# Where the sums of weights of the fifth and sixth slot are made, in a two-layer decoder trunk in fp32

## The chip, the cores and the metric

One core of one Trainium2 chip runs the kernel. The metric is the device time of one execution in microseconds (us). About 0.2% of it (1.8 us) is what a measurement of this kernel can tell from no change.

## What is computed

The reference is a decoder trunk with two layers on 256 tokens of width 1024, all in float32. Each layer is

```python
x = x + 0.5 * swiglu(rmsnorm(x, norm_ffn1[l]), ffn1_w_in[l], ffn1_w_out[l])
z = rmsnorm(x, norm_mix[l]) @ mix_w_in[l]
...
x = x + y @ mix_w_out[l]
x = x + 0.5 * swiglu(rmsnorm(x, norm_ffn2[l]), ffn2_w_in[l], ffn2_w_out[l])
```

where `swiglu(h, w_in, w_out)` is `(silu(g) * u) @ w_out` with a hidden width of 2816. The change lies in the last product of a layer, `(silu(g) * u) @ ffn2_w_out[l]`: 256 x 2816 by 2816 x 1024.

## The kernel before, in words

**Split products.** TensorE multiplies in a reduced format, so each fp32 operand is split into a rounded part and a remainder (`w_hi`, `w_lo`), and each product is three matmuls (`three`, lines 500 to 503). ScalarE makes the rounded parts (`w_hi` at L1016, or L1007 for a wide tile; `h_hi` at L1089; `s_hi` at L994), VectorE the remainders (`w_lo` at L1324 or L1319, `h_lo` at L1445, `s_lo` at L1348, `hs_lo` at L1452), each by a subtraction that needs the rounded part.

**Order of the work.** Each engine walks through the same half-steps h of a stage (4 to 4·UB+FT+1 with UB = 11 and FT = 22: the first 44 belong to the up product, the rest to the down product). At each h, VectorE does in this order: a `hidden` pair, if due; the remainder of a weight tile (`split`); a remainder of sums (`sums_split`); sums of weights (`sums_make`); `sums_lo`; `hidden_lo`. Tables of half-steps (`LOAD_AT`, `SUMS_AT`, `SPLIT_AT`, `HIDDEN_AT`, lines 46 and 75 to 79) say when each is due. Weights come through SP's DMA queue into three `raw` buffers; the load of tile n waits until VectorE has made the remainder of tile n-3 (`room`, L333). `w_hi` and `w_lo` have four places each (RING), and ScalarE waits for TensorE to free one.

**Seven products in place of eight.** In ffn2's down product six pairs of rows ("slots" 3 to 8 of 11, `SEVEN`; m counts them, six a layer) are multiplied by seven block products in place of eight. That needs four sums of weight blocks, T1 to T4, each 128x512, and four sums of hidden blocks, S1 to S4 (`sums_a`, then `hs_hi`, `hs_lo`). For the sums of weights the slot's weights are loaded a second time, unsplit, into an area (`load_sums`, L375 to L390): slots one to four of the six use areas 0 and 1 (`sums_b`), the fifth area 2 and the sixth area 3 (tiles `area0`, `area1`, which lie where `x_hi` and `x_lo` are). The loads of the fifth and sixth are issued at half-steps 52 and 54 in SP's order, which is ahead of the others. VectorE makes the four sums in place one after the other, each after the one before (L1334, L1336, L1338, L1340; `sb_done` counts them), at h = 53 for the fifth and h = 56 for the sixth slot. ScalarE rounds the whole area (`sums_split`, L994; it waits for `sb_done` and for TensorE to be through with the s buffer before), and VectorE makes `s_lo` (L1348).

**TensorE** in `seven_rows` (L729): waits for the slot's `w_lo` (L759), does three products with plain blocks, then waits for `slo_done` (L763) and does four with summed blocks. Ahead of the first of the six slots it waits for all of `h_lo` and for `hs_lo` (L786, L787).

**GpSimd** runs the small work of the state-space group (tables, powers of the mean squares) with each of its instructions behind the one before. In each layer its last step of `mix` is `norm(norm_no(l, 2))`; its next is the norm of the following layer (L1898), or at the end L1905.

Of the kernel before, what the change touches and what calls it, by code (L numbers as in the profile page):

```python
# [11 lines left out]
ALU = mybir.AluOpType  # L12
# [7 lines left out]
UB = FF // 256  # L20
# [52 lines left out]
N7 = len(SEVEN)  # L73

AREA = (0, 1, 0, 1, 2, 3)
LOAD_AT = (26, 28, 36, 38, 4 * UB + 8, 4 * UB + 10)
SUMS_AT = (25, 29, 36, 41, 4 * UB + 9, 4 * UB + 12)
SPLIT_AT = (28, 31, 4 * UB + 11, 4 * UB + 13, 4 * UB + 15, 4 * UB + 17)
FOLD_AT = 4 * UB + 2 * SEVEN[-1] + 5

# [1 line left out]
T3, T1, T2, T4 = range(4)  # L82
# [11 lines left out]
def half(l, h):  # L94
    return l * HALVES + h
# [18 lines left out]
def norm_no(l, i):  # L114
    return 3 * l + i
# [23 lines left out]
def build(nc, a, out):  # L139
    stack = ExitStack()  # L140
    with stack:
# [3 lines left out]
        def sem(name):  # L145
            return stack.enter_context(nc.semaphore(name))
# [53 lines left out]
        with ExitStack() as second_use:  # L200
            areas = [second_use.enter_context(nc.sbuf_tensor(f"area{t}", [P, 2048], F32))[:, :] for t in range(2)]
        x_hi = sb("x_hi", [P, KT, L], F32R)
        x_lo = sb("x_lo", [P, KT, L], F32R)
        areas = [sums_b[:, 0, :], sums_b[:, 1, :]] + areas
# [71 lines left out]
        sb_done, p1_done, fold_done = sem("sb_done"), sem("p1_done"), sem("fold_done")  # L276
# [24 lines left out]
        def sums_full(m):  # L301

            i = m % N7
            uses = [q for q in range(N7) if AREA[q] == AREA[i]]
            return s_full[AREA[i]], ((m // N7) * len(uses) + uses.index(i) + 1) * 32
# [5 lines left out]
        def hidden_bank(l, j, b):  # L311

            c0, _, t0, t1_ = ROLES[l, stage_of(2 * j)]
            if b == UB - 1:
                return bank[2 * c0]
            return bank[2 * (t1_ if b in (2, 3, 6, 7) else t0) + b % 2]

        def gate_bank(l, i, f):
            c0, c1, _, _ = ROLES[l, "mix"]
            return bank[2 * (c0, c1)[i // 2] + i % 2][:, f * L:f * L + L]  # L320
# [176 lines left out]
        def _(pe):  # L497
# [231 lines left out]
            def seven_rows(l, i, h, k, pairs, extra):  # L729
# [4 lines left out]
                for kk in range(2):  # L734
                    for t in range(2):
                        tok = slice(t * P, t * P + P)
                        a_hi.append(h_hi[:, k + kk, tok])
                        a_lo.append(h_lo[:, k + kk, tok])
                a11, _, a12, a22 = range(4)
                for q in range(4):  # L740
                    a_hi.append(hs_hi_of(i)[:, q * P:q * P + P])
# [564 lines left out]
        def _(dve):  # L1306
# [19 lines left out]

            def sums_make(l, h):

                for i in range(N7):
                    if SUMS_AT[i] == h:  # L1330
                        m = l * N7 + i
                        q = areas[AREA[i]].rearrange("p (i m) -> p i m", i=4)
                        dve.wait_ge(*sums_full(m))
                        TT(q[:, T1, :], q[:, 0, :], q[:, T1, :], ALU.subtract).then_inc(sb_done, 1)  # L1334
                        dve.wait_ge(sb_done, 4 * m + 1)
                        TT(q[:, T3, :], q[:, 0, :], q[:, 2, :], ALU.subtract).then_inc(sb_done, 1)  # L1336
                        dve.wait_ge(sb_done, 4 * m + 2)
                        TT(q[:, T2, :], q[:, 2, :], q[:, T1, :], ALU.subtract).then_inc(sb_done, 1)  # L1338
                        dve.wait_ge(sb_done, 4 * m + 3)
                        TT(q[:, T4, :], q[:, 3, :], q[:, T2, :], ALU.subtract).then_inc(sb_done, 1)  # L1340
# [134 lines left out]
            def ffn(l, j):  # L1475
                f = 2 * l + j
                if f == 0:
                    first_in()
                elif j == 0:
                    norm_in(l, 0, UPS[j], ACC_FFN2, (0.5, 0.5), DN2 + FT - 1)  # L1480
                else:
                    norm_in(l, 2, UPS[j], ACC_SSM, (ors[:, 2:3], ors[:, 3:4]), OUT + KT - 1)
                for h in range(4 if f else 5, 4 * UB + FT + 1):
                    if h in GATES_AT[f]:
                        hidden(l, j, GATES_AT[f][h])
                    split(l, UPS[j] + h)
                    if j:
                        sums_split(l, h)
                        sums_make(l, h)
                    if j and h - 1 in HIDDEN_AT and HIDDEN_AT.index(h - 1) in SEVEN:  # L1490
                        sums_lo(l, HIDDEN_AT.index(h - 1))
                    if h in HIDDEN_AT:
                        hidden_lo(l, j, HIDDEN_AT.index(h))
                    if j and h == FOLD_AT:
                        fold(l, j)
# [146 lines left out]
        def _(pool):  # L1642
            steps = [0]

            def link(ins):
                steps[0] += 1
                ins.then_inc(pool_chain, 1)
                pool.wait_ge(pool_chain, steps[0])

            def restart():  # L1650
                steps[0] = 0
                pool.sem_clear(pool_chain)

            def tt(o, x0, x1, op):
                link(nc.gpsimd.tensor_tensor(o, x0, x1, op))  # L1655
# [7 lines left out]
            def inv_sqrt(o, m, done):  # L1663
                ins = nc.gpsimd.tensor_tensor(o, m, neg_half[:, 0:1].broadcast_to([P, m.shape[1]]), ALU.pow)  # L1664
                ins.then_inc(done, 1)

            def norm(n):
                pool.wait_ge(ms_done, n + 1)
                inv_sqrt(rstd_c[:, :], ms_c[:, :], rstd_done)
# [170 lines left out]
            def mix(l):  # L1840
                c = slice(1, NC + 1)
                norm(norm_no(l, 1))
                pool.wait_ge(half_done, half(l, DN1 + FT - 1) + 1)
                link(nc.gpsimd.memset(h_re[:, :, 0:1], 0.0))
                nc.gpsimd.memset(h_im[:, :, 0:1], 0.0).then_inc(ku_done, 1)
                for hf in range(2):
                    q = slice(8 * hf, 8 * hf + 8)
                    pool.wait_ge(rot_done, l * 8 + 4 * hf + 2)
                    nc.gpsimd.tensor_tensor(t1[:, q, :], t1[:, q, :], t3[:, q, :], ALU.add).then_inc(turn_done, 1)
                    pool.wait_ge(rot_done, l * 8 + 4 * hf + 4)  # L1850
                    nc.gpsimd.tensor_tensor(t2[:, q, :], t2[:, q, :], h_re[:, q, c], ALU.subtract).then_inc(turn_done, 1)

                def state(hf):
                    q = slice(8 * hf, 8 * hf + 8)
                    pool.wait_ge(un_done, l * 8 + 4 * hf + 2)
                    nc.gpsimd.tensor_tensor(h_re[:, q, c], h_re[:, q, c], t2[:, q, :], ALU.subtract).then_inc(re_done, 1)
                    pool.wait_ge(un_done, l * 8 + 4 * hf + 4)
                    nc.gpsimd.tensor_tensor(h_im[:, q, c], h_im[:, q, c], t3[:, q, :], ALU.add).then_inc(im_done, 1)

                pool.wait_ge(vsq_done, l + 1)  # L1860
                for t in range(2):
                    nc.gpsimd.tensor_tensor(vg[:, t, :], vg[:, t, :], vgain[:, :], ALU.mult).then_inc(vgm_done, 1)
                pool.wait_ge(vms_done, l + 1)
                for t in range(2):
                    heads = slice(t * HEADS, t * HEADS + HEADS)
                    inv_sqrt(vrs[:, heads], vms[:, heads], vrs_done)
                state(0)
                state(1)
                pool.wait_ge(oms_done, l * 2 + 1)
                inv_sqrt(ors[:, 0:2], oms[:, 0:2], ors_done)  # L1870
                pool.wait_ge(osq_done, l + 1)
                tt(vn[:, 0, :], vn[:, 0, :], vn[:, 1, :], ALU.add)
                nc.gpsimd.tensor_tensor(vn[:, 0, 0:L], vn[:, 0, 0:L], vn[:, 0, L:2 * L], ALU.add).then_inc(oadd_done, 1)
                pool.wait_ge(oms_done, l * 2 + 2)
                inv_sqrt(ors[:, 2:4], oms[:, 2:4], ors_done)
                norm(norm_no(l, 2))

            link(nc.gpsimd.memset(ident[:, :], 0.0))
            link(nc.gpsimd.affine_select(out=ident[:, :], in_=ident[:, :], compare_op=ALU.not_equal, fill=1.0,
                                         base=0, pattern=[[-1, P]], channel_multiplier=1))  # L1880
# [14 lines left out]
            prep_rest(0)  # L1895
            restart()
            mix(0)
            norm(norm_no(1, 0))  # L1898
            pool.wait_ge(half_done, half(1, 0))
            clear_blocks()  # L1900
# [1 line left out]
            prep_rest(1)  # L1902
            restart()
            mix(1)
            pool.wait_ge(ms_done, 3 * DEPTH + 1)  # L1905
            inv_sqrt(rstd_c[:, 0:1], ms_c[:, 0:1], rstd_done)
            pool.wait_ge(x_done, residuals(DEPTH - 1, ACC_FFN2) + 3)
# [22 lines left out]
```

## Time and profile before

| what | value |
|---|---|
| median of 3 runs | 908.31 us (908.05 to 908.76) |
| the profiled execution | 907.8 us, its span 906.1 us |
| TensorE matmul busy | 897.4 us, 99% of the span |
| VectorE busy | 620.3 us, 68% |
| ScalarE busy | 507.4 us, 56% |
| GpSimd busy | 371.8 us, 41% |
| mean granted TensorE clock | 0.999 |

The span is the time from the first instruction to the last; the execution's own time is 1.7 us more. Busy time of TensorE is modelled for each matmul and matmuls overlap, so stalls are looked for in the waits and in the pitch of the weight loads (PEld). "a <- b" in a list of waits says that a's engine stood idle until b was done. The timeline gives start, duration, engine and line, and in brackets the idle time before. Two instructions one behind the other on VectorE can overlap by some 0.08 us in it.

### The profile page before, as it was taken

How to read it: one execution, taken by the hardware profiler on the slowest of the kernel's cores; microseconds unless marked ns; L12 is line 12 of the kernel's file. 1: busy time of each engine (PE TensorE's matmuls, PEld its weight loads, DVE VectorE, ACT ScalarE, POOL GpSimd, SP SyncE). 2: the span in 40 equal slices, each digit the busy share in tenths (PEclk: the TensorE clock that was granted, in tenths of full speed). 3: DMA queues.
4: the chain of work that ended last, by engine and by line, in shares of the span. 5: the costliest groups of instructions: out<-in, count | busy, mean ns of one | idle time of the engine just before them, and what ended most of it. 6: DMA issues, size and time to landing. Idle time of an engine off the chain costs nothing.

```text
span 906.1 us, 12882 instructions
## 1 busy us (share of the span) xinstructions
PE 897.4 (99%) x4935; PEld 743.1 (82%) x4935; DVE 620.3 (68%) x729; ACT 507.4 (56%) x741; POOL 371.8 (41%) x574
## 2 busy tenths in 40 slices
PE   9999999999999999999999999999999999999997
PEld 7888888888878888887888888888888888888886
DVE  5555665458976578868965656653888855789597
ACT  6544454458766456646464445445677654656474
POOL 3488999894510000000055889988734100000000
PEclk9999999999999999999999999999999999999999
DMA  9786555544256677684559665555344476785751
GB/s 281 196 271 188 186 184 180 175 160 142 94 194 200 196 251 230 229 283 159 186 175 246 186 188 186 186 186 186 120 160 143 139 221 196 263 270 188 267 175 46
DMA packets 138381, 174.60 MB, mean 193 GB/s; under 512 B 18760, under 2 KB 110032, under 8 KB 138320
## 3 DMA queue, kind: packets, MB, share of 16 engines
q1 hardware_dynamic: 138032, 173.24, 59.7%
q8 instruction: 39, 0.64, 0.3%
q10 hardware_dynamic: 288, 0.53, 0.2%
q14 instruction: 22, 0.18, 0.1%
HBM read 172.70 MB, written 1.05 MB: 192 GB/s over the span
## 4 chain that ended last, share of the span: by engine, by line
PE 95%; DVE 3%; issue 1%; DMA 1%; ACT 1%; SPq 0%; ACTq 0%; DVEq 0%
PE bank L501 29%; PE bank L503 29%; PE bank L502 29%; PE bank L606 2%; DVE w_lo L1319 1%; PE bank L511 1%; PE bank L833 1%; DVE s_lo L1348 1%; DMA raw<-in_ffn_w_in 1%; PE bank L861 0%; PE bank L851 0%; PE bank L874 0%; PE bank L716 0%; ACT w_hi L1007 0%; PE bank L937 0%
## 5 line engine op out<-in xcount | busy, mean ns | idle before, releaser
L1324 DVE TENSOR_TENSOR w_lo<-raw,w_hi 128x1024 fp32r<-128x1024 f32 x278 | 351.0, 1271 | 214.4 <-ACT w_hi L1016 214.2
L1016 ACT ACTIVATE w_hi<-raw 128x1024 fp32r<-128x1024 f32 x278 | 292.7, 1061 | 242.0 <-PE bank L503 223.2
L501 PE MATMUL bank<-w_hi,x_hi 128*128 128x512 f32 x856 | 336.5, 393 | 0.0
L503 PE MATMUL bank<-w_hi,x_lo 128*128 128x512 f32 x856 | 333.5, 390 | 0.0
L502 PE MATMUL bank<-w_lo,x_hi 128*128 128x512 f32 x856 | 333.2, 389 | 0.0
L501 PEld LDWEIGHTS bank<-w_hi,x_hi 128*128 128x128 f32 x856 | 160.7, 188 | 35.2 <-issue 2.5
L503 PEld LDWEIGHTS bank<-w_hi,x_lo 128*128 128x128 f32 x856 | 160.7, 188 | 33.7
L502 PEld LDWEIGHTS bank<-w_lo,x_hi 128*128 128x128 f32 x856 | 160.8, 188 | 32.3
L1664 POOL TENSOR_TENSOR rstd_c<-ms_c,neg_half 128x2 f32<-128x2 f32 (+1 forms) x7 | 7.7, 1106 | 394.9 <-DVE ms_c L1367 394.9
L501 PE MATMUL bank<-w_hi,h_hi 128*128 128x512 f32 (+1 forms) x283 | 111.0, 392 | 0.0
L503 PE MATMUL bank<-w_hi,h_lo 128*128 128x512 f32 (+1 forms) x283 | 109.7, 387 | 0.0
L502 PE MATMUL bank<-w_lo,h_hi 128*128 128x512 f32 (+1 forms) x283 | 109.6, 387 | 0.0
L1079 ACT ACTIVATE sil<-bank,rstd_c 128x256 f32<-128x256 f32 x88 | 36.8, 470 | 53.2 <-PE bank L503 53.1
L501 PEld LDWEIGHTS bank<-w_hi,h_hi 128*128 128x128 f32 x283 | 53.1, 188 | 11.4 <-DVE h_lo L1445 0.6
L503 PEld LDWEIGHTS bank<-w_hi,h_lo 128*128 128x128 f32 x283 | 53.1, 188 | 11.0
L502 PEld LDWEIGHTS bank<-w_lo,h_hi 128*128 128x128 f32 x283 | 53.2, 188 | 10.4
L1655 POOL TENSOR_TENSOR sc<-sc 128x16 f32<-128x16 f32 (+1 forms) x154 | 55.2, 358 | 12.3
L1428 DVE SCALAR_TENSOR_TENSOR hid<-bank,rstd_c,sil 128x256 f32<-128x256 f32 x88 | 38.5, 479 | 24.4 <-ACT sil L1079 24.4
L1655 POOL TENSOR_TENSOR pt<-sc,bp 128x256 f32<-128x256 f32 x56 | 52.6, 940 | 4.4
L1658 POOL TENSOR_SCALAR sc<-sc 128x16 f32<-128x16 f32 (+1 forms) x90 | 38.7, 430 | 7.7
L1655 POOL TENSOR_TENSOR bp<-pt 128x256 f32<-128x256 f32 x32 | 36.3, 1133 | 2.5
L1319 DVE TENSOR_TENSOR w_lo<-raw,w_hi 128x1536 fp32r<-128x1536 f32 x12 | 21.0, 1753 | 12.9 <-ACT w_hi L1007 12.9
(231 smaller groups left out, 886.9 us busy)
## 6 DMA issues: line engine op xcount, KB each, us to landing
raw<-in_ffn_w_in SPq DMA_DIRECT2D x172, 512.0 KB
raw<-in_ffn_w_out SPq DMA_DIRECT2D x32, 1024.0 KB
raw<-in_mix_w_in SPq DMA_DIRECT2D x12, 1024.0 KB
raw<-in_mix_w_out SPq DMA_DIRECT2D x8, 1024.0 KB
sums_b<-in_ffn_w_out SPq DMA_DIRECT2D x16, 512.0 KB, 6.9
raw<-in_ffn_w_out SPq DMA_DIRECT2D x12, 512.0 KB
area<-in_ffn_w_out SPq DMA_DIRECT2D x8, 512.0 KB, 6.4
raw<-in_ffn_w_out SPq DMA_DIRECT2D x12, 256.0 KB
```

The lines of the kernel that those rows point to most:

```text
L501: mm(o, hi_a, hi_b, start=first, stop=False)
L502: mm(o, hi_a, lo_b, start=False, stop=False)
L503: return mm(o, lo_a, hi_b, start=False, stop=last)
L511: ins = nc.tensor.transpose(turned(pair, j)[:, h * P:h * P + P], x[:, h, k * P:k * P + P], ident[:, :])
L606: ins = nc.tensor.transpose(hidden_bank(l, j, b)[:, c:c + P], hid[:, b % 4, h, ft * P:ft * P + P], ident[:, :])
L1016: A(w_hi[:, n % RING, :], raw[:, s, (n % 2) * 1024:(n % 2) * 1024 + 1024], ACT.Copy).then_inc(hi_done, 1)
L1079: A(sil[:, b % 2, t, :], bank[2 * pair + t][:, 0:256], ACT.Silu, scale=rstd_c[:, t:t + 1]).then_inc(sil_done, 1)
L1319: TT(w_lo[:, n % RING:n % RING + 2, :].rearrange("p s m -> p (s m)")[:, 0:1536], raw[:, s, 0:1536], w_hi[:, n % RING:n % RING + 2, :].rear ...
L1324: TT(w_lo[:, n % RING, :], raw[:, s, (n % 2) * 1024:(n % 2) * 1024 + 1024], w_hi[:, n % RING, :].bitcast(F32), ALU.subtract).then_inc(lo_d ...
L1428: STT(hid[:, b % 4, t, :], bank[2 * pair + t][:, 256:512], rstd_c[:, t:t + 1], sil[:, b % 2, t, :], ALU.mult, ALU.mult).then_inc(hid_done, 1)
L1655: link(nc.gpsimd.tensor_tensor(o, x0, x1, op))
L1658: link(nc.gpsimd.tensor_scalar(o, x0, s1, s2, op0, op1))
```

## The change

The table `SUMS_AT` loses its two last entries, so VectorE makes the sums of the first four of the six slots only. GpSimd gets a function of its own that makes those of the fifth and the sixth, with the same four subtractions in the same order, eight a layer, called behind `mix(l)`. Each of its four waits for the one before; the first waits for all sums of earlier slots (`sb_done`) and for the slot's loads. The loads, the rounding on ScalarE, `s_lo` on VectorE and all of TensorE's program stay.

```diff
-SUMS_AT = (25, 29, 36, 41, 4 * UB + 9, 4 * UB + 12)
+SUMS_AT = (25, 29, 36, 41)
...
             def sums_make(l, h):
 
-                for i in range(N7):
+                for i in range(len(SUMS_AT)):
                     if SUMS_AT[i] == h:
...
+            def sums_make(l):
+
+                for i in range(len(SUMS_AT), N7):
+                    m = l * N7 + i
+                    q = areas[AREA[i]].rearrange("p (i m) -> p i m", i=4)
+                    pool.wait_ge(sb_done, 4 * m)
+                    pool.wait_ge(*sums_full(m))
+                    nc.gpsimd.tensor_tensor(q[:, T1, :], q[:, 0, :], q[:, T1, :], ALU.subtract).then_inc(sb_done, 1)
+                    pool.wait_ge(sb_done, 4 * m + 1)
+                    nc.gpsimd.tensor_tensor(q[:, T3, :], q[:, 0, :], q[:, 2, :], ALU.subtract).then_inc(sb_done, 1)
+                    pool.wait_ge(sb_done, 4 * m + 2)
+                    nc.gpsimd.tensor_tensor(q[:, T2, :], q[:, 2, :], q[:, T1, :], ALU.subtract).then_inc(sb_done, 1)
+                    pool.wait_ge(sb_done, 4 * m + 3)
+                    nc.gpsimd.tensor_tensor(q[:, T4, :], q[:, 3, :], q[:, T2, :], ALU.subtract).then_inc(sb_done, 1)
...
             mix(0)
+            sums_make(0)
             norm(norm_no(1, 0))
...
             mix(1)
+            sums_make(1)
             pool.wait_ge(ms_done, 3 * DEPTH + 1)
```

## Rows read from the trace of the kernel before

**Rows 1.** The page: busy time of each engine, and its chain that ended last.
```profile
PE 897.4 (99%) x4935; PEld 743.1 (82%) x4935; DVE 620.3 (68%) x729; ACT 507.4 (56%) x741; POOL 371.8 (41%) x574
...
PE 95%; DVE 3%; issue 1%; DMA 1%; ACT 1%; SPq 0%; ACTq 0%; DVEq 0%
```

**Rows 2.** Waits of the whole span: total in us, times, longest.
```profile
PEld bank L501 <- DVE s_lo L1348: 1.5, 2, 0.7
...
PEld bank L501 <- DVE h_lo L1445: 0.6, 2, 0.3
```

**Rows 3.** Timeline, TensorE's weight loads in the six slots of layer 0.
```profile
412.91 0.19 PEld L503 LDWEIGHTS bank<-w_hi,h_lo 128*128 128x128 f32 x1
...
415.36 0.19 PEld L501 LDWEIGHTS bank<-s_hi,hs_hi 128*128 128x128 f32 x1
...
429.41 0.19 PEld L503 LDWEIGHTS bank<-w_hi,h_lo 128*128 128x128 f32 x1
...
432.98 0.19 PEld L501 LDWEIGHTS bank<-w_hi,h_hi 128*128 128x128 f32 x1
...
437.74 0.19 PEld L501 LDWEIGHTS bank<-w_hi,h_hi 128*128 128x128 f32 x1
```

**Rows 4.** Timeline, VectorE from 402 us (layer 0), and one of layer 1.
```profile
402.41 1.23 DVE L1324 TENSOR_TENSOR w_lo<-raw,w_hi 128x1024 fp32r<-128x1024 f32 x1 [1.44 <-ACT w_hi L1016]
...
409.79 1.76 DVE L1319 TENSOR_TENSOR w_lo<-raw,w_hi 128x1536 fp32r<-128x1536 f32 x1 [4.58 <-ACT w_hi L1007]
411.47 0.68 DVE L1452 TENSOR_TENSOR hs_lo<-sc,hs_hi_last 128x512 fp32r<-128x512 f32 x1
412.07 1.28 DVE L1445 TENSOR_TENSOR h_lo<-bank,h_hi 128x512 fp32r<-128x512 f32 x2
...
416.90 0.69 DVE L1334 TENSOR_TENSOR area<-area 128x512 f32<-128x512 f32 x1
...
425.23 0.68 DVE L1334 TENSOR_TENSOR area<-area 128x512 f32<-128x512 f32 x1
...
428.01 2.28 DVE L1348 TENSOR_TENSOR s_lo<-sums_b,s_hi 128x2048 fp32r<-128x2048 f32 x1
...
856.09 1.76 DVE L1319 TENSOR_TENSOR w_lo<-raw,w_hi 128x1536 fp32r<-128x1536 f32 x1 [4.58 <-ACT w_hi L1007]
```

**Rows 5.** Timeline, ScalarE: the rounding of the fourth and the fifth slot's sums.
```profile
423.32 1.93 ACT L994 ACTIVATE s_hi<-sums_b 128x2048 fp32r<-128x2048 f32 x1 [1.20 <-PE bank L503]
...
428.08 1.92 ACT L994 ACTIVATE s_hi<-area 128x2048 fp32r<-128x2048 f32 x1 [1.21 <-DVE area L1340]
```

**Rows 6.** Loads into the two areas, layer 0: issues (duration, starts), then landing.
```profile
L390 SPq DMA_DIRECT2D area<-in_ffn_w_out x2: 368/420/471, 395.9 to 396.3; - x2
...
DMA to landing us min/median/max: 4.8/5.4/6.0
...
L390 SPq DMA_DIRECT2D area<-in_ffn_w_out x2: 432/450/469, 399.9 to 400.3; - x2
...
DMA to landing us min/median/max: 5.8/6.3/6.8
```

**Rows 7.** GpSimd's groups by shape: count, busy us, mean ns.
```profile
L1849 POOL TENSOR_TENSOR t<-t 128x512 f32<-128x512 f32 x4 | 5.2, 1291 | 17.4 <-DVE t L1516 17.4
...
L1851 POOL TENSOR_TENSOR t<-t,h_re 128x512 f32<-128x512 f32 x4 | 4.8, 1202 | 0.0
```

**Rows 8.** Timeline of layer 0's mixing stage: VectorE, then GpSimd beside it.
```profile
229.10 0.69 DVE L1534 TENSOR_TENSOR t<-t,sinn 128x512 f32<-128x512 f32 x1
...
237.06 1.51 DVE L1533 TENSOR_TENSOR h_re<-t,cosn 128x512 f32<-128x512 f32 x1
238.49 1.67 DVE L1534 TENSOR_TENSOR t<-t,sinn 128x512 f32<-128x512 f32 x1
...
236.47 1.54 POOL L1856 TENSOR_TENSOR h_re<-h_re,t 128x512 f32<-128x512 f32 x1
237.98 1.63 POOL L1858 TENSOR_TENSOR h_im<-h_im,t 128x512 f32<-128x512 f32 x1
```

## Prediction

> **What bounds the kernel now.** I read the page first: TensorE is busy 99% of the span and makes up 95% of the chain that ended last [rows 1]. VectorE, at 68%, can only matter where TensorE stands still for it. So the list of waits comes next, and it holds just two kinds in which TensorE waits for VectorE in the last product of a layer, each twice, once a layer [rows 2]: for `s_lo`, 0.7 us each, and for `h_lo`, 0.3 us each. Everything the change can give or take has to pass through one of these two.
>
> What they cost is read from the pitch of the weight loads. From 432.98 to 437.74 there are 21 loads without a stall, 0.2267 us each [rows 3]. From 429.41 to 432.98 there are 13, which at that pitch take 2.95 us and took 3.57: the wait for `s_lo` costs **0.62 us** a layer. From 412.91 to 415.36 there are 10, 2.27 us at that pitch against 2.45: the wait for `h_lo` costs 0.18 us, less than its idle time, as queued matmuls catch up in part. The waits have the same lengths in both layers [rows 2], so I take layer 0's figures twice.
>
> Then the timeline of VectorE says what is in front of either wait. In front of `s_lo` of the fourth slot (428.01 to 430.29, and TensorE's load follows at once) VectorE works without a break from 416.90 on, and in that stretch lie both groups of sums, from 416.90 and from 425.23 [rows 4]. In front of `h_lo` (412.07 to 413.35) lie `w_lo` at 409.79, which started as soon as ScalarE's `w_hi` allowed (4.58 us of idle before it), and `hs_lo` at 411.47 [rows 4]. The sums are not in front of this one today.
>
> **Taken from VectorE.** Four subtractions a slot, two slots a layer: 8 a layer, 0.69 us each [rows 4], 5.5 us a layer, 11 us in all. Nearly all of this is off TensorE's path; what it is worth is the wait for `s_lo`. The second group alone runs from 425.23 to 428.01, 2.8 us right ahead of the late `s_lo`. Without the groups that `s_lo` follows its rounded part, which ends at 423.32 + 1.93 = 425.25 [rows 5]; it would end near 425.3 + 2.3 = 427.6, where TensorE asks for it at about 429.6 (429.41 and one pitch) [rows 3]. That leaves 2 us of room, so the 0.62 us go entirely: **-1.24 us** for two layers. What is late next? ScalarE's rounding for the fifth slot waited for the sums (428.08) [rows 5], but in that moment TensorE is also just through with the buffer it needs, so it hardly moves, and TensorE has no wait for the `s_lo` behind it in the list [rows 2]. I take no further gain. The weight tiles whose remainders come earlier let SP issue loads up to 2 us earlier; TensorE waits for no load here, so I cost this at nothing, covered by the three-deep ring.
>
> **Added to GpSimd.** 8 subtractions of 128x512 a layer. GpSimd's own of this shape take 1.20 and 1.29 us where nothing disturbs them [rows 7], and 1.54 to 1.63 beside VectorE's [rows 8]. With a wait between them I take a pitch of 1.3 to 1.4 us, as an estimate from these. It is idle in this stretch, and its own next work comes only in the next layer. The fifth slot's loads are down at 396.3 + 6.0 = 402.3, the sixth's at 400.3 + 6.8 = 407.1 [rows 6]. Eight subtractions from 402.3 on end between 413 and 416.5. The first consumer, ScalarE's rounding, asks at 428: more than 11 us of cover, so the slower engine itself costs nothing. If the cover went, each microsecond late would be one lost on ScalarE and then on TensorE. DMAs are neither added nor moved, and the waits put nothing behind them but the next norm.
>
> **The price: the two engines side by side.** This is where the sum is decided. GpSimd now works from 402 to about 415, and in that stretch lies the chain to `h_lo`, which has no room at all, since TensorE waits for it already. What does a GpSimd subtraction do to one of VectorE's? The same VectorE line, 128x512, took 0.69 us at 229.10 with GpSimd idle and 1.67 us at 238.49 with one of GpSimd's 128x512 under way, and the one in front of it 1.51 us [rows 8]: 0.83 to 0.99 us more. The GpSimd instructions there started at 236.47 and 237.98, so the two engines took turns, and two VectorE instructions in a row were held, each by another of GpSimd's [rows 8]. Both read their two inputs from SBUF. `w_lo` (raw, w_hi) and `hs_lo` (sc, hs_hi_last) do as well; `h_lo` has one input in a PSUM bank and I count it unheld.
>
> Now the phase. `w_lo` at 402.41 holds GpSimd's first subtraction until 403.6; four of them end at 408.7 to 409.1, and the fifth, whose data are down since 407.1, lasts until 410.0 to 410.4. `w_lo` asks at 409.79 and is held for 0.2 to 0.6 us: I take 0.35. During it the sixth queues up and goes first when it ends, so `hs_lo` is held like 238.49: 0.95. Together **1.3 us** more for TensorE's wait for `h_lo` in layer 0; layer 1's `w_lo` stands at the same place of its stage, 856.09 [rows 4], and I take the same: +2.6 us. The bounds: nothing, if GpSimd happens not to hold them; 2 x 0.99 = 1.98 a layer, if `w_lo` comes just behind the start of one of GpSimd's. Later VectorE work is free of it, GpSimd being done by 416.5.
>
> The Trainium skill, "SBUF — State Buffer", section "Who interferes with whom", has it that a VectorE instruction with two SBUF inputs and a GpSimd instruction that reads SBUF exclude each other for the whole instruction, and the later one fully blocks. That agrees with [rows 8] in kind and speaks against this change. Taken by its word, `hs_lo` would be held for a whole GpSimd subtraction, 1.20 us in place of 0.95, and the sum below would be +1.9 in place of +1.4, 910.2 us; the held rows decide for me.
>
> **Sum.** -1.24 + 2.6 = **+1.4 us**. The profiled execution of 907.8 us (span 906.1 and 1.7 around it) would become 909.2; the median of the runs is 908.31, 0.5 us above the profiled one, so the forecast for the median is **909.7 us**, +0.15%. A measurement of this kernel tells about 0.2%, 1.8 us, from no change: below 906.5 is faster, above 910.1 slower.
>
> **Rivals.**
>
> *The worst phase at h_lo (slower).* One mechanism: `w_lo` of the first slot asks just after GpSimd has begun a subtraction, waits out nearly all of it, and `hs_lo` waits out the next. Price 1.98 us a layer, 2 x (1.98 - 0.62) = +2.7, 911.0 us. It decides from 0.62 + 0.91 = 1.53 us of hold a layer on. For it: a pitch of only 0.1 us less or more over five subtractions shifts the phase by half of one. Against it: both my ends of the pitch put `w_lo` near the end of the fifth. The Trainium skill's page on SBUF, in the section named above, would allow 1.20 for each hold and 911.9 us by this mechanism. Chance 0.25.
>
> *No collision on the path (the gain stands).* GpSimd is between two subtractions when `w_lo` and `hs_lo` come, or VectorE is served first; then the -1.24 stands, 907.1 us, -0.14%: still within 0.2%. For it: each of GpSimd's subtractions here waits for the one before, so there are gaps in which VectorE may slip in. Against it: in [rows 8] VectorE was held twice in a row. Chance 0.12.
>
> *GpSimd is late for ScalarE.* The fifth slot's four would have to last from 402.3 to past 428 [rows 5, 6], over 6 us each, four times the slowest of [rows 8]. Then the sums stay the last wait and each microsecond counts twice. Chance 0.02, 912 us or more.
>
> *The change does not do what it says.* It moves eight subtractions a layer and no others, and nothing forces VectorE to wait for GpSimd except through ScalarE. That it leaves VectorE's order untouched, so that the wait for `s_lo` stays, would give +2.6 us; the room of 2 us speaks against it. Chance 0.03.
>
> **How the numbers follow.** The forecast has 0.58 and spans 908.6 to 910.3 by itself. Slower by over 0.2% gets the worst phase (0.25), the two small rivals in most part (0.04) and the forecast's top (0.03): 0.32. Faster needs a gain beyond the 1.24 us that the two `s_lo` waits hold, plus the 0.36 of the `h_lo` waits, 1.6 together and still short of 1.8: 0.04. The rest, 0.64, is within 0.2%. The range reaches from the full gain, 907.1, down by a little for the run's spread, to the worst phase: 907.0 to 911.2.
>
> **What would show it.** In the changed kernel's waits: `s_lo` gone from those TensorE waits for, and `h_lo` grown from 0.3 to about 1.6 us each. In VectorE's timeline: the first wide `w_lo` of each layer 2.0 to 2.4 us long in place of 1.76, the last `hs_lo` 1.5 to 1.7 in place of 0.68. In GpSimd's: sixteen subtractions on `area`, 1.2 to 1.8 us each, done by 416.5 and, 446.3 us later like `w_lo`, by 863. ScalarE's rounding of the fifth slot waits for TensorE. VectorE's busy time falls by 11 less some 2.6. Wrong I am if `h_lo`'s wait stays at 0.3 us, if `s_lo`'s stays, or if a third wait of TensorE appears.

## The result, and the profile after

The changed kernel takes **910.18 us** (median of 13 runs, 908.90 to 912.34) against 908.13 us (13 runs, 907.74 to 908.93): a ratio of 1.0021 (95% interval 1.0013 to 1.0030), 1.9 us slower by the ratio, 2.05 us between the medians. The forecast was 909.7 us. The runs of the changed kernel are also spread three times as wide. Two executions further down, one of e6 (1124.31 us) and one of e7 (1394.66 us), ran at a mean granted clock of 0.753 and 0.605 against 0.998 and more in the others of these two kernels, and are left out of their ranges and ratios.

The page of its profile (span 908.0 us) first: busy time by engine. Sixteen instructions have left VectorE and sixteen have come to GpSimd.

```profile
PE 896.7 (99%) x4935; PEld 742.8 (82%) x4935; DVE 615.6 (68%) x713; ACT 507.5 (56%) x741; POOL 396.8 (44%) x590
```

VectorE's busy time has fallen by 4.7 us [rows 1], though sixteen subtractions of 0.69 us are 11: most of the rest has come back as holds (`w_lo` and `hs_lo` took longer by 5.2 us over the span, of which 2.7 us lie in front of `h_lo`). The list of waits (total, times, longest) shows where they reach TensorE:

```profile
PEld bank L501 <- DVE h_lo L1445: 3.3, 2, 1.9
...
PE bank L501 <- DVE h_lo L1445: 2.5, 2, 1.5
```

TensorE's wait for `s_lo` [rows 2] is gone from the list, and that for `h_lo` has grown from 0.3 to 1.9 us in layer 0 and 1.4 us in layer 1. Timeline of VectorE and, below it, of GpSimd, in front of this wait in layer 0:

```profile
410.26 2.29 DVE L1319 TENSOR_TENSOR w_lo<-raw,w_hi 128x1536 fp32r<-128x1536 f32 x1 [4.58 <-ACT w_hi L1007]
412.48 1.78 DVE L1452 TENSOR_TENSOR hs_lo<-sc,hs_hi_last 128x512 fp32r<-128x512 f32 x1
414.18 1.27 DVE L1445 TENSOR_TENSOR h_lo<-bank,h_hi 128x512 fp32r<-128x512 f32 x2
415.69 2.68 DVE L1319 TENSOR_TENSOR w_lo<-raw,w_hi 128x1536 fp32r<-128x1536 f32 x1 [0.24 <-ACT w_hi L1007]
```

```profile
404.19 1.29 POOL L1885 TENSOR_TENSOR area<-area 128x512 f32<-128x512 f32 x1 [125.27 <-DMA area<-in_ffn_w_out]
...
409.64 1.29 POOL L1885 TENSOR_TENSOR area<-area 128x512 f32<-128x512 f32 x1
411.02 2.69 POOL L1887 TENSOR_TENSOR area<-area 128x512 f32<-128x512 f32 x1
413.78 1.61 POOL L1889 TENSOR_TENSOR area<-area 128x512 f32<-128x512 f32 x1
```

Against [rows 4], `w_lo` is held for 0.53 us (2.29 against 1.76) by the fifth GpSimd subtraction, and `hs_lo` for 1.10 (1.78 against 0.68) by the sixth, which itself had stood behind `w_lo` (2.69 us long, where an undisturbed one takes 1.29). The two `h_lo`, one input in PSUM, keep 1.27. A hold has further consequences only where TensorE waits: the next `w_lo`, 2.68 us, leads to no wait of TensorE. Layer 1:

```profile
857.55 1.76 DVE L1319 TENSOR_TENSOR w_lo<-raw,w_hi 128x1536 fp32r<-128x1536 f32 x1 [3.61 <-ACT w_hi L1007]
859.23 1.78 DVE L1452 TENSOR_TENSOR hs_lo<-sc,hs_hi_last 128x512 fp32r<-128x512 f32 x1
```

```profile
856.35 1.29 POOL L1885 TENSOR_TENSOR area<-area 128x512 f32<-128x512 f32 x1
857.72 2.74 POOL L1887 TENSOR_TENSOR area<-area 128x512 f32<-128x512 f32 x1
```

Here `w_lo` asked at 857.55, when the fifth was all but over (857.64), and was not held; `hs_lo` was, by 1.10 again.

**What TensorE loses.** As in the prediction, the loss is the time from one weight load to a later one less their number times 0.2267 us. For the kernel after, in layer 0:

```profile
413.38 0.19 PEld L503 LDWEIGHTS bank<-w_hi,h_lo 128*128 128x128 f32 x1
...
417.46 0.19 PEld L501 LDWEIGHTS bank<-s_hi,hs_hi 128*128 128x128 f32 x1
```

Ten loads in 4.08 us lose 1.81 us; layer 1 loses 1.27. Before it was 0.18 + 0.62 = 0.80 in each [rows 3]. So the change costs 1.01 + 0.47 = 1.5 us here. The other 0.4 to 0.5 us between the two profiled spans (908.0 and 906.1) lie ahead of the change: `w_lo` at 410.26 in place of 409.79 has the same 4.58 us of idle before it; such shifts come and go between executions (in the twelve traces of this document this `w_lo` starts between 409.48 and 411.72 us).

### The profile page after: what moved, and what is told of

It is laid out like the page before. It is cut to its first block, busy times and chain, and to the rows that moved or that the text cites. A ratio compares the mean times of both kernels' runs of the same rounds, so it can differ in the third digit from the quotient of the medians.

```text
span 908.0 us, 12886 instructions
## 1 busy us (share of the span) xinstructions
PE 896.7 (99%) x4935; PEld 742.8 (82%) x4935; DVE 615.6 (68%) x713; ACT 507.5 (56%) x741; POOL 396.8 (44%) x590
## 4 chain that ended last, share of the span: by engine, by line
PE 97%; DVE 1%; DMA 1%; ACT 1%; issue 0%; SPq 0%; ACTq 0%; DVEq 0%
PE bank L501 30%; PE bank L503 30%; PE bank L502 30%; PE bank L606 2%; PE bank L511 1%; PE bank L833 1%; DMA raw<-in_ffn_w_in 1%; PE bank L861 0%; PE bank L851 0%; DVE w_lo L1319 0%; PE bank L874 0%; PE bank L716 0%; DVE hs_lo L1452 0%; ACT w_hi L1007 0%; PE bank L937 0%; DVE h_lo L1445 0%
## 5 line engine op out<-in xcount | busy, mean ns | idle before, releaser
L1885 POOL TENSOR_TENSOR area<-area 128x512 f32<-128x512 f32 x4 | 5.2, 1292 | 249.2 <-DMA area<-in_ffn_w_out 249.0
L1655 POOL TENSOR_TENSOR sc<-sc 128x16 f32<-128x16 f32 (+1 forms) x154 | 59.1, 384 | 12.3
L1658 POOL TENSOR_SCALAR sc<-sc 128x16 f32<-128x16 f32 (+1 forms) x90 | 34.2, 380 | 7.7
```

The costliest lines, as they stand in the source:

```text
L1658: link(nc.gpsimd.tensor_scalar(o, x0, s1, s2, op0, op1))
```

## The experiments

Ten kernels. Each was compared with the kernel before on the same chip: 908.08 us for the first four, 907.91 for the next four, 907.88 for the last two. The gains below, 1.1 to 1.6 us, are less than the 1.8 us that one measurement of this kernel tells from no change; they are read from the intervals of the ratios and from the waits in the traces together.

**e1: both slots behind h_lo.** The changed kernel with

```diff
                     pool.wait_ge(sb_done, 4 * m)
+                    pool.wait_ge(hlo_done, UB * (2 * l + 1) + UB)
```

> The changed kernel, but GpSimd waits for the stage's last h_lo before its eight subtractions, so that none lies beside w_lo and hs_lo. Theory (the two engines take turns, and what is lost is lost in front of h_lo): TensorE's wait for h_lo back at 0.3 us, the wait for s_lo stays gone, so before less 2 x 0.62: about 906.9 us against 908.1. GpSimd ends eight subtractions by about 413.4 + 8 x 1.4 to 1.6 = 424.5 to 426, ahead of the 430 at which ScalarE asks. Rival (GpSimd's subtractions cost time wherever they stand, as they hold VectorE's w_lo and s_lo there too, or come late for ScalarE): 908.5 us or more, with a new wait for w_lo or s_lo in TensorE's list.

Measured: 910.14 us (909.83 to 911.67), ratio 1.0024 (1.0014 to 1.0035). The wait for `h_lo` is back at 0.3 us, and the time is not. VectorE, then GpSimd, then the waits:

```profile
424.15 2.85 DVE L1319 TENSOR_TENSOR w_lo<-raw,w_hi 128x1536 fp32r<-128x1536 f32 x1
426.93 3.37 DVE L1348 TENSOR_TENSOR s_lo<-sums_b,s_hi 128x2048 fp32r<-128x2048 f32 x1
```

```profile
425.47 2.69 POOL L1888 TENSOR_TENSOR area<-area 128x512 f32<-128x512 f32 x1
428.24 3.22 POOL L1890 TENSOR_TENSOR area<-area 128x512 f32<-128x512 f32 x1
431.54 2.69 POOL L1892 TENSOR_TENSOR area<-area 128x512 f32<-128x512 f32 x1
```

```profile
ACT s_hi L994 <- POOL area L1892: 4.4, 2, 2.2
PEld bank L501 <- DVE s_lo L1348: 3.3, 4, 1.3
```

My expectation was wrong. VectorE hardly pauses here, and the engines take turns: each `w_lo` and `s_lo` stands for one GpSimd subtraction (`s_lo` 3.37 us, 2.28 alone), and after the first two, which took 1.30 us, each GpSimd subtraction for one of VectorE's (2.69 to 3.23 us). GpSimd needs 20.3 us for its eight, and at last ScalarE waits for them. TensorE loses 1.77 us a layer: some 0.2 at `h_lo` as before, and nearly all of the rest at `s_lo` of the fourth and of the fifth slot, for which VectorE's held work makes it wait. ScalarE's wait for the sixth slot does not reach TensorE, which has no wait for that slot's `s_lo`. The rival that the subtractions cost time wherever they stand holds for eight of them in this stretch.

**e2: the sixth slot behind h_lo, the fifth at once.** As e1, with `if i == N7 - 1:` ahead of the wait.

> The changed kernel, but only the sixth slot's four subtractions wait for the stage's last h_lo; the fifth's run as soon as their data are down, from about 403 to 409.2. Theory: they end ahead of w_lo's start near 409.8, so h_lo's wait is back at 0.3 us and the time is e1's, about 906.9 us, with GpSimd done earlier (about 419). If the fifth's last subtraction now and then reaches into w_lo, up to 0.3 us a layer more in single executions. Rival (the fifth slot's subtractions are what holds the chain): h_lo's wait stays above 1 us and the time near 910.

Measured: 906.75 us (906.26 to 907.73), ratio 0.9987 (0.9979 to 0.9996). The theory holds: the fifth's last subtraction ends at 409.57, `w_lo` follows at 410.85 unheld, and the sixth's four take 8.2 us. They end at 422.8 and not at about 419 as I had expected, still ahead of ScalarE. VectorE, then GpSimd:

```profile
410.85 1.76 DVE L1319 TENSOR_TENSOR w_lo<-raw,w_hi 128x1536 fp32r<-128x1536 f32 x1 [3.57 <-ACT w_hi L1007]
```

```profile
408.28 1.29 POOL L1893 TENSOR_TENSOR area<-area 128x512 f32<-128x512 f32 x1
...
420.06 2.69 POOL L1893 TENSOR_TENSOR area<-area 128x512 f32<-128x512 f32 x1
```

**e3: the reads alone.** The kernel before, VectorE making all sums, with on GpSimd behind `mix(l)`

```diff
+                for i in (4, 5):
+                    pool.wait_ge(*sums_full(l * N7 + i))
+                    for _ in range(4):
+                        tt(own, own, own, ALU.subtract)
```

where `own` is a 128x512 piece of `gfin` (layer 0) or `pad` (layer 1) that nothing else needs then; a memset fills it first.

> The kernel before, VectorE making all sums, with eight GpSimd subtractions of 128x512 on a tile of its own (both inputs in SBUF, nothing else uses them) at the moments at which the changed kernel makes its own. Theory (the hold alone): the price without the gain, so h_lo's wait at 1.4 to 1.9 us as in the changed kernel, s_lo's wait still there: 2 x 1.2 to 1.6 over before, 910.5 to 911.4 us. GpSimd's later ones also meet sums on VectorE and may lengthen the s_lo chain by up to 0.5 a layer. Rival (the price is in the areas themselves, bank or address conflicts with the loads and with ScalarE): 908.1 us, h_lo's wait 0.3.

Measured: 909.29 us (908.38 to 910.50), ratio 1.0014 (1.0005 to 1.0023). That is 1.2 us short of the 910.5 to 911.4 that I expected, but far above the rival's 908.1: the hold comes with subtractions that touch no area. It is smaller, and so are these: 1.04 us undisturbed, with inputs and output the same piece, and `hs_lo` was held for 0.84 us (1.52 against 0.68).

```profile
410.64 1.95 DVE L1319 TENSOR_TENSOR w_lo<-raw,w_hi 128x1536 fp32r<-128x1536 f32 x1 [4.58 <-ACT w_hi L1007]
412.51 1.52 DVE L1452 TENSOR_TENSOR hs_lo<-sc,hs_hi_last 128x512 fp32r<-128x512 f32 x1
```

```profile
L1655 POOL TENSOR_TENSOR gfin<-gfin x8: 1040/1041/2434, 403.8 to 413.6; 128x512 f32<-128x512 f32 x8
```

The part that I had not expected: **TensorE's wait for `s_lo` is gone here too**, though no sum has left VectorE. Of the two waits in this product only the one for `h_lo` is left:

```profile
PEld bank L501 <- DVE h_lo L1445: 2.5, 2, 1.3
```

```profile
429.06 2.28 DVE L1348 TENSOR_TENSOR s_lo<-sums_b,s_hi 128x2048 fp32r<-128x2048 f32 x1
```

The second row, from the timeline, is the `s_lo` that TensorE used to wait for. It starts 18.4 us behind the `w_lo` of 410.64, against 18.2 before (409.79 and 428.01 [rows 4]), so VectorE's chain has hardly moved; TensorE comes later by what it lost at `h_lo`, and its load follows at 431.52, 0.18 us after `s_lo` is done.

**e4: writes in place of reads.** As e3, with ten `link(nc.gpsimd.memset(own, 1.0))` a slot.

> As e3, but in place of the eight subtractions twenty GpSimd memsets of 128x512 (writes, no reads), about 0.5 us each and one behind the other over the same stretch. Theory (what is taken in turns is the second input's read): w_lo and hs_lo keep 1.76 and 0.68 us, h_lo's wait 0.3, time 908.1 us. Rival (any GpSimd instruction on SBUF holds VectorE): w_lo and hs_lo held by up to 0.5 us each, 909 to 910 us.

Measured: 908.19 us (907.49 to 909.83), ratio 1.000 (0.9991 to 1.0009). Nothing is held, with GpSimd busy from 405.6 to past 416:

```profile
411.72 1.76 DVE L1319 TENSOR_TENSOR w_lo<-raw,w_hi 128x1536 fp32r<-128x1536 f32 x1 [4.58 <-ACT w_hi L1007]
413.40 0.68 DVE L1452 TENSOR_TENSOR hs_lo<-sc,hs_hi_last 128x512 fp32r<-128x512 f32 x1
```

```profile
L1883 POOL MEMSET gfin<- x20: 524/526/528, 405.6 to 416.7; 128x512 f32 x20
```

**e5: hs_lo behind h_lo.** The changed kernel; on VectorE the last slot's `sums_lo` moves from ahead of the last two `hidden_lo` to behind them.

```diff
-                    if j and h - 1 in HIDDEN_AT and HIDDEN_AT.index(h - 1) in SEVEN:
+                    if j and h - 1 in HIDDEN_AT[:SEVEN[-1]] and HIDDEN_AT.index(h - 1) in SEVEN:
                         sums_lo(l, HIDDEN_AT.index(h - 1))
                     if h in HIDDEN_AT:
                         hidden_lo(l, j, HIDDEN_AT.index(h))
+                    if j and h == HIDDEN_AT[-1]:
+                        sums_lo(l, SEVEN[-1])
```

> The changed kernel, with VectorE making the last slot's hs_lo behind the stage's last two h_lo in place of ahead of them (TensorE needs it only 25 us later). Theory (the price is the hold of w_lo and of hs_lo in front of h_lo, and hs_lo's part is the larger): h_lo then follows w_lo, its wait for TensorE falls from 1.4 to 1.9 us to 0 to 0.3 us, and with s_lo's wait still gone the time is 908.1 - 2 x 0.62 - 0.36 + 0 to 0.5 = 906.5 to 907.0 us. Rival (w_lo's hold carries the price): 908.5 us or more.

Measured: 906.71 us (906.30 to 908.20), ratio 0.9987 (0.9979 to 0.9996). One instruction less in the chain turns the change from a loss into a gain, with GpSimd's work where the change has it. TensorE waits for neither `h_lo` nor `s_lo`, although `w_lo` was held (2.08 us long):

```profile
410.50 2.08 DVE L1319 TENSOR_TENSOR w_lo<-raw,w_hi 128x1536 fp32r<-128x1536 f32 x1 [4.58 <-ACT w_hi L1007]
412.50 1.28 DVE L1445 TENSOR_TENSOR h_lo<-bank,h_hi 128x512 fp32r<-128x512 f32 x2
```

**e7: the same move in the kernel before.**

> The kernel before with nothing but hs_lo moved behind h_lo; VectorE makes all sums. Theory (the chain to s_lo on VectorE does not shift when TensorE stands for h_lo, so a stall in front of h_lo is taken off the later one for s_lo, as e3 suggests): h_lo's wait goes and s_lo's grows by the same 0.2 us, the time stays 908.1 us. Rival (the two waits add, as my sum has it): 908.1 - 0.36 = 907.7 us with s_lo's wait unchanged at 0.7 us.

Measured: 907.94 us (907.34 to 908.47; 907.91 before), ratio 0.9998 (0.9989 to 1.0007). `h_lo` is gone from TensorE's waits, and the one for `s_lo` has grown from 0.7 [rows 2] to 0.9 us:

```profile
PEld bank L501 <- DVE s_lo L1348: 1.9, 2, 0.9
```

```profile
428.24 2.28 DVE L1348 TENSOR_TENSOR s_lo<-sums_b,s_hi 128x2048 fp32r<-128x2048 f32 x1
```

The losses a layer are 0.79 and 0.84 us, as before the move. This `s_lo` again starts 18.2 us behind the wide `w_lo` (at 410.03 here): VectorE's chain does not shift, and when TensorE comes to it earlier, it waits longer. So the two waits do not add. The medians alone could hardly tell this from the rival's 907.7; the waits do.

**e8: only the fifth slot on GpSimd.** `SUMS_AT` keeps 4·UB+12 for the sixth slot on VectorE, which waits there for GpSimd's four; GpSimd's loop is `for i in (4,)`.

> GpSimd makes the sums of the fifth slot only, VectorE keeps those of the sixth at their old place. Theory: GpSimd is done by about 409.2, ahead of w_lo, so nothing is held; VectorE's chain to s_lo is 2.8 us shorter, but then waits for ScalarE twice, and s_lo ends at about 429.5, just where TensorE asks for it: h_lo's wait 0.3 us, s_lo's at most 0.1, time 906.9 to 907.1 us. Rival (both groups must leave VectorE for the s_lo wait to go): 907.5 to 908.1 us with s_lo's wait at 0.4 to 0.7.

Measured: 906.77 us (906.21 to 907.67), ratio 0.9985 (0.9976 to 0.9994). Half of the change gives all of the gain that there is at `s_lo`:

```profile
426.25 0.69 DVE L1342 TENSOR_TENSOR area<-area 128x512 f32<-128x512 f32 x1
426.86 2.28 DVE L1350 TENSOR_TENSOR s_lo<-sums_b,s_hi 128x2048 fp32r<-128x2048 f32 x1
```

```profile
407.28 1.29 POOL L1893 TENSOR_TENSOR area<-area 128x512 f32<-128x512 f32 x1
```

GpSimd is through at 408.57, 0.9 us ahead of `w_lo` (409.48). `s_lo` starts 1.15 us earlier than in [rows 4], 0.8 us beyond the 0.31 us by which `w_lo` is earlier too, and that is more than the 0.62 us that TensorE had lost.

**e6: e2 and e5 together.**

> e2 (only the sixth slot's sums wait for the last h_lo) and hs_lo behind h_lo together. Theory: both waits of TensorE for VectorE in this product are gone, 1.6 us in all off before: 906.4 to 906.5 us, the fastest of all. Rival (something else holds TensorE as soon as these are gone): 906.8, e2's time, or more.

Measured: 906.36 us (905.92 to 906.77), ratio 0.9981 (0.9972 to 0.9990), the fastest. TensorE loses nothing in this product in either layer. From e2, e5 and e8 its distance is within what the runs can tell.

**e9 and e10: the phase by hand.** The phase is the point within one of GpSimd's subtractions at which VectorE's `w_lo` asks. The changed kernel, with GpSimd's first subtraction of a layer tied to a moment of VectorE's; e10 has the last line as well.

```diff
                     pool.wait_ge(sb_done, 4 * m)
+                    if i == len(SUMS_AT):
+                        pool.wait_ge(hlo_done, UB * (2 * l + 1) + 9)
+                        link(nc.gpsimd.memset((gfin[:, 0:512], pad[:, 0:512])[l], 1.0))
```

> The changed kernel, with GpSimd's first subtraction of a layer tied to VectorE's h_lo of the ninth hidden tile (it ends 4.6 us ahead of the wide w_lo) in place of the landing of the loads alone. Theory (the hold is set by where in one of GpSimd's subtractions w_lo asks): the fourth starts some 0.4 us ahead of w_lo, which is held for 0.7 to 0.9 us, and hs_lo for 1.1: h_lo's wait 2.1 to 2.3 us in both layers, time 910.6 to 911.2, and a spread much narrower than the changed kernel's 908.9 to 912.3. Rival (landing moments have nothing to do with the spread): the same median and spread as the changed kernel.

> As e9, with one memset of 128x512 (0.5 us) on GpSimd between the anchor and the first subtraction, so that all of them lie 0.6 us later against w_lo. Theory: w_lo asks just as the third ends and is held 0 to 0.2 us, hs_lo still 1.1: h_lo's wait 1.4 to 1.6 us, time 909.3 to 909.7, 1.2 to 1.5 us below e9 though GpSimd does more and later. Rival (later work on GpSimd can only cost more): at or above e9.

Measured: e9 911.76 us (910.17 to 912.23, five executions only), ratio 1.0038 (1.0024 to 1.0051); e10 909.16 us (908.36 to 910.59), ratio 1.0015 (1.0006 to 1.0024). e9 lies above the 910.6 to 911.2 that I expected, e10 a little below 909.3. With 0.5 us more of work in front, e10 is 2.6 us faster; 1.5 us of that is the difference of the two layers' holds of `w_lo`, and the clock, told of below, has a share in the rest. First e9 (VectorE, GpSimd), then e10:

```profile
409.55 2.57 DVE L1319 TENSOR_TENSOR w_lo<-raw,w_hi 128x1536 fp32r<-128x1536 f32 x1 [4.58 <-ACT w_hi L1007]
...
409.21 1.30 POOL L1893 TENSOR_TENSOR area<-area 128x512 f32<-128x512 f32 x1
```

```profile
410.22 1.80 DVE L1319 TENSOR_TENSOR w_lo<-raw,w_hi 128x1536 fp32r<-128x1536 f32 x1 [4.58 <-ACT w_hi L1007]
...
409.11 1.29 POOL L1892 TENSOR_TENSOR area<-area 128x512 f32<-128x512 f32 x1
```

In e9 `w_lo` asks 0.34 us into a subtraction and is held for 0.81; in e10 it asks 0.18 us ahead of the end of one and is held for 0.04. The spread did not become "much narrower" in e9 (2.1 us against 3.4 of the changed kernel's 13; e10 2.2 in 11), so the landing moments are at most part of it; what the rest is stays open. And e9 lost more than its holds: in layer 1 TensorE stood for 2.22 us, worked for 1.3 us, and then its granted clock fell. Weight loads there, and the stretch from 860 to 865 us (columns: busy time and count of PE, PEld, DVE, ACT, POOL; granted clock; DMA share; GB/s):

```profile
863.92 0.29 PEld L501 LDWEIGHTS bank<-w_hi,h_hi 128*128 128x128 f32 x1
864.30 0.33 PEld L502 LDWEIGHTS bank<-w_lo,h_hi 128*128 128x128 f32 x1
864.73 0.33 PEld L503 LDWEIGHTS bank<-w_hi,h_lo 128*128 128x128 f32 x1
```

```profile
860.00:865.00 5.00, 3.20 (x12) 2.31 (x11) 4.31 (x4) 1.48 (x1) 4.84 (x3) 0.89 0.50 157
```

The granted clock of this stretch is 0.89 and of the next, 865 to 870 us, 0.76: each is a mean over time at 2.4 GHz and time at the lower of the two levels, 1.2 GHz. Eight loads go at a pitch of 0.38 to 0.43 us, nearly twice the usual one, before 0.23 returns: 1.6 us lost on top of the 2.1 of the stall. The stall of the same length in layer 0 had no such sequel (granted clock 1.00 throughout), and no run here shows why the one had it and the other not.

**The losses side by side.** What TensorE lost in layers 0 and 1 by the pitch of its loads, the change of their sum against before (1.60), and the change of the medians:

| kernel | lost, us | sum - 1.60 | medians |
|---|---|---|---|
| after | 1.82, 1.27 | +1.5 | +2.1 |
| e1 | 1.77, 1.78 | +2.0 | +2.1 |
| e2 | 0.22, 0.22 | -1.2 | -1.3 |
| e3 | 1.22, 1.04 | +0.7 | +1.2 |
| e4 | 0.79, 0.84 | 0.0 | +0.1 |
| e5 | 0.03, 0.03 | -1.5 | -1.2 |
| e6 | 0.00, 0.00 | -1.6 | -1.6 |
| e7 | 0.79, 0.84 | 0.0 | 0.0 |
| e8 | 0.19, 0.19 | -1.2 | -1.1 |
| e9 | 2.10, 3.72 | +4.2 | +3.9 |
| e10 | 1.35, 1.33 | +1.1 | +1.3 |

The left side is one execution, the right one five to thirteen; they agree within 0.6 us, less than executions of one kernel differ by (the kernel before took 907.74 to 908.93).

## Why the prediction was right

**The sum** was +1.4 us, +0.15%; measured +1.9, +0.21%. Its own measure, the losses in the profiled execution, gives +1.5. The measured time lies inside the range. It also lies just above 910.1, the prediction's own mark for "slower", to which it gave 0.32, and so not in the 0.64 of "within 0.2%"; the interval of the ratio, 1.0013 to 1.0030, covers both sides of the mark.

**The place** is as forecast: TensorE's wait for `s_lo` gone, that for `h_lo` grown. The fall of VectorE's busy time was put at 11 less 2.6, some 8.4 us, and was 4.7: the holds off TensorE's path had been left out of that. e5 shows that the chain in front of `h_lo` carries the whole price: with `hs_lo` out of it and all else as in the change, 910.18 becomes 906.71.

**The hold** was put at 0.35 for `w_lo` and 0.95 for `hs_lo`. Measured were 0.53 and 0.00 for `w_lo` in the two layers and 1.10 for `hs_lo` in both. The mean of the layers, 1.37, is near my 1.3 by luck, for two errors went against each other: `hs_lo`'s term was short, as GpSimd's subtractions here take 1.29 us and not 1.20, and `w_lo`'s phase was a draw, which e9 (0.81) and e10 (0.04) turn by hand. The later one of the two was held for the time that the earlier one still had to go, less 0.14 to 0.2 us: 1.10 for 1.29 and, in e3, 0.84 for 1.04 (`hs_lo`); 0.53 for 0.67 and, in e9, 0.81 for 0.96 (`w_lo`). The Trainium skill, "SBUF — State Buffer", section "Who interferes with whom", has the later one block fully. The runs bear that out in kind; 1.10 lies between the 1.29 that a full block would make of it and my 0.95.

**The step that failed though the total stood** is "-1.24": that relieving VectorE brings 1.24 us, set off against 2.6 for the holds. e8 shows the gain to be real by itself (0.19 lost in place of 0.80). But the two do not add. e3 loses `s_lo`'s wait without any relief, because TensorE, held at `h_lo`, comes to `s_lo` later than the unshifted chain on VectorE; e7 is the same seen from the other side. In the changed kernel the relief was worth next to nothing: a loss of 0.80 at two points became one of 1.3 to 1.8 at the first, and the second would have vanished anyway. That is shown by e3 for its own, smaller holds; for the changed kernel it is an estimate, and a close one: TensorE comes to `s_lo` 1.63 us later in layer 0, less the 0.62 that it had lost there and the 0.92 by which the second wide `w_lo` was held, which leaves 0.1. The sum came out right only because both ways of counting take 0.62 off.

**The cover of GpSimd** was right for the change (done at 416.8 us, while ScalarE's rounding starts at 430.2) and would not have been for a later place. I wrote that later VectorE work is free of GpSimd; it was not (`w_lo` 2.68 us), and e1 shows what that costs when the stretch has no pauses.

**The rivals.** The worst phase is nearly what e9 made: 3.9 us over before, against my 2.7. In its profiled execution TensorE lost 4.2 us more than before, 2.6 by the holds and 1.6 by the clock, which the prediction did not have. The gain without collision is e2 and e8: 1.3 and 1.1 us, against my 1.24. The changed kernel's slowest run, 912.34, is beyond what the holds give. It has no trace, but its mean granted clock is 0.997, the lowest of the 13 (the others 0.998 to 1.000) and the same as in e9's profiled run; that the clock fell in it as in e9 is likely, not shown.

## What to carry to other kernels

Before an elementwise operation goes to an idle GpSimd, list VectorE's instructions with two SBUF inputs in the stretch where it will run, and look at each with no room: one held in front of a critical wait cost up to about a GpSimd instruction's length here (1.10 us of 1.29), however idle both engines look in the sum. The smaller move can be the better one: half of this change, or the whole of it with one non-urgent VectorE instruction taken out of the critical chain, gained 1.1 to 1.2 us where the change lost 1.9. And two waits of one engine on another in a row are not to be added before it is asked whether a longer first one eats the second.

## What was new about the hardware

- Of GpSimd's instructions it is those that read which held VectorE here: twenty GpSimd memsets of 128x512 a layer left VectorE's two-input subtractions at 1.76 and 0.68 us (e4), eight subtractions stretched them to 1.95 and 1.52 (e3). VectorE's `h_lo`, with one input in PSUM, kept 1.27 us beside a GpSimd subtraction (the changed kernel).
- A VectorE subtraction that came later was held for the time that GpSimd's still had to go, less 0.14 to 0.2 us (1.10 for 1.29, 0.84 for 1.04).
- With work queued on both, the engines took turns, one instruction each: eight GpSimd subtractions of 1.29 us took 20.3 us, and VectorE's `s_lo` 3.37 in place of 2.28 (e1).
- A GpSimd subtraction of 128x512 took 1.04 us with inputs and output the same piece (e3) and 1.28 to 1.30 on the areas, with two different inputs; another line of this shape took 1.20 [rows 7].
- Of two stalls of TensorE of 2.22 us in e9's trace one was followed by a fall of the granted clock, 0.89 and 0.76 over two stretches of 5 us, and by 1.6 us more of loss.
